# Loading order at the start of two stages of a hybrid decoder step: channel constants laid out on the host, weights in column halves, rows and tables ahead of the rest

## What is computed

```python
# layer 0: top-k sparse attention and retention side by side
qa, ka, va, iq, ik, iw, za, qb, kb, vb, zb = ab_project(rmsnorm(ys, norm_w[layer]), pos_s, w_in_ab[j])
oa = dsa_sample(qa, ka, va, iq, ik, iw, cache_k[j], cache_v[j], cache_kidx[j], page_table, topk_s)
ob, r_new = retention_chunked(qb, kb, vb, state_ret[j])
ys = ys + ab_output(oa, za, ob, zb, gn_ret[j], w_out_ab[j])
...
# layer 1: projection, causal convolution of width 4, gated delta rule
qkv, z, a, b = _split(h @ w_in, C_SIZES)
qkv, conv_new = causal_conv(qkv, conv_prefix, conv_w)
...
o = rmsnorm(o, gdn_norm) * jax.nn.silu(z.reshape(Bn, T, C_V_HEADS, C_V_DIM).astype(F32))
y = o.reshape(Bn, T, C_WIDTH).astype(h.dtype) @ w_out
```

## Time and profile before

| | us |
|---|---|
| median of 3 runs | 4261.64 |
| lowest, highest | 4259.95, 4264.33 |
| the profiled execution's own time | 4269.43 |
| its span | 4267.8 |
| PE busy | 3495.6 (82%) |
| DVE busy | 1880.5 (44%) |
| ACT busy | 1390.1 (33%) |
| POOL busy | 860.0 (20%) |

### The profile page before, as it was taken

How to read it: one execution, slowest core, us unless ns; L and a number is a source line. 1 busy time by engine, 2 the same in 40 slices (tenths; PEclk the granted TensorE clock), 3 DMA queues, 4 the chain that set the end, 5 groups by cost and what they waited for, 6 DMA issues and landing times. The chain is left out here.

```text
span 4267.8 us, 47903 instructions
## 1 busy us (share of the span) xinstructions
PE 3495.6 (82%) x15465; PEld 2026.5 (47%) x15465; DVE 1880.5 (44%) x3884; ACT 1390.1 (33%) x2831; POOL 860.0 (20%) x1709
## 2 busy tenths in 40 slices
PE   7999548899898988866538978979989864997998
PEld 4445334455555555653214434434434444665665
DVE  0000056677777775326400331521502436674664
ACT  2111135566565756522101111111111113442442
POOL 3112253221121100000000000000000004775572
PEclk9999778999999996877768989989989886998999
DMA  7333225454333320024041011010110113322321
GB/s 238 103 107 121 89 88 163 146 156 128 113 118 104 107 63 3 3 83 168 0 175 55 29 50 49 27 61 34 33 58 32 46 38 111 103 85 86 127 75 60
DMA packets 239806, 366.62 MB, mean 86 GB/s; under 512 B 54628, under 2 KB 139661, under 8 KB 235437
## 3 DMA queue, kind: packets, MB, share of 16 engines
q1 hardware_dynamic: 215920, 334.62, 24.2%
q10 hardware_dynamic: 19584, 21.05, 1.4%
q0 software_dynamic: 4096, 8.40, 0.7%
HBM read 279.22 MB, written 106.04 MB: 90 GB/s over the span
## 5 line engine op out<-in xcount | busy, mean ns | idle before, releaser
L1898 PE MATMUL QB<-hT,w_c 128*128 128x512 f32 (+1 forms) x1280 | 480.0, 529 | 0.0
L328 PE MATMUL P0A<-w_all,hT 128*128 128x512 f32 (+1 forms) x1200 | 432.9, 522 | 0.0
L631 PE MATMUL PB<-wb,hT_ahead 128*128 128x512 f32 x704 | 367.1, 648 | 3.4 <-ACT prb L751 1.9
L655 PEld LDWEIGHTS PO<-vst,ptT 128*128 128x128 f32 x2176 | 294.8, 207 | 81.0 <-issue 43.1
L1898 PEld LDWEIGHTS QB<-hT,w_c 128*128 128x128 f32 x1280 | 220.3, 191 | 218.1 <-issue 218.1
L655 PE MATMUL PO<-vst,ptT 128*128 128x64 f32 x2176 | 308.3, 287 | 13.4 <-ACT ptT L771 13.1
L328 PEld LDWEIGHTS P0A<-w_all,hT 128*128 128x128 f32 x1200 | 207.9, 191 | 220.5 <-issue 220.5
L2148 POOL TENSOR_SCALAR stat<-stat 128x1 f32<-128x1 f32 x17 | 3.3, 191 | 1438.6 <-POOLq L120 1438.6
L1864 PE MATMUL QS<-w_o,yT 128*128 128x512 f32 x544 | 277.3, 674 | 11.5 <-ACT yT L1996 11.5
L642 PE MATMUL PT<-ident,sm 128*128 128x128 f32 x1088 | 198.2, 308 | 106.1 <-ACT sm L763 105.9
L1887 PE MATMUL QA<-w_c,hT 128*128 128x512 f32 (+1 forms) x816 | 274.6, 493 | 9.3 <-ACT hT L2011 9.3
(11 more groups left out here) (404 smaller groups left out, 5253.0 us busy)
## 6 DMA issues: line engine op xcount, KB each, us to landing
wb<-in_w_in_ab SPq DMA_DIRECT2D x176, 512.0 KB, 3.7
out_c_all<-crow SPq DMA_DIRECT2D x272, 64.0 KB, 1.7
w_c<-in_w_in_c ACTq DMA_DIRECT2D x8, 1544.0 KB, 17.8
w_all<-in_w_in_ab SPq DMA_DIRECT2D x48, 256.0 KB, 8.0
out_pr_all<-pr_out SPq DMA_DIRECT2D x17, 546.0 KB, 2.9
pra<-out_pr_all SPq DMA_DIRECT2D x16, 546.0 KB, 4.6
x_rows<-in_x_all SPq DMA_DIRECT2D x17, 512.0 KB, 6.0
yab<-out_yab_all SPq DMA_DIRECT2D x17, 512.0 KB, 3.8
```

The costliest lines, as they stand in the source:

```text
L328: ins = pe.matmul(PA[u % 6][:, 0:b - a], hT[:, t % (LAG + 2), c, :], w_all[:, c, a:b], start=(c == 0), stop=(c == KD - 1))
L631: ins = pe.matmul(PB[:, :], hT[:, 2 * q + k, :], wb[:, u % 4, k, :], start=(q == 0 and k == 0), stop=(q == 3 and k == 1))
L655: ins = pe.matmul(PO[:, h * HD:(h + 1) * HD], ptT[:, v % 2, k * P:(k + 1) * P], vst[:, 4 * c + k, a * HD:(a + 1) * HD], start=(c == 0 and ...
L1898: ins = pe.matmul(PB[b % 2][:, 0:N], w_c[:, c, b * P:(b + 1) * P], hT[:, c, 0:N], start=(c == 0), stop=(c == KD - 1))
```

## The change

In the sample stage the rows, the two rotary tables and the identity are loaded first, under a semaphore of their own (rows4_loaded); PE, ACT and DVE start on that. The index blocks follow, then the other 12 constants under c4_loaded, for which DVE now waits after rope4 (the scaling of gng moves there too), and PE before its attention scores.

In the conv stage the host hands over nw1, gn and cw in the layout of their tiles. They are loaded first with ident, then yab and xin of sub-tile 0, then w_o in 16 pieces: eight for the left 512 columns (w2o_loaded0), eight for the right (w2o_loaded1). ACT waits for the right half and issues w_c in 16 pieces: the gate columns (w2z_loaded), then the rest (w2c_loaded). SP's sub_in(T) becomes next_in(T), which loads yab and xin of sub-tile T+1 as soon as T has used the buffers, ahead of the stores of T.

```diff
@@ layer0_samples, sync
+            rows = ((pr[:, :], io["pr_all"][SEQ:ROWS, :]),
+                    (ropea.rearrange("p a h d -> p (a h d)"), io["ropea"][SEQ:ROWS, :]),
+                    (ropeb.rearrange("p a d -> p (a d)"), io["ropeb"][SEQ:ROWS, :]), (ident[:, :], io["ident"]))
...
+            for dst, src in rows:
+                sp.dma_start(dst, src).then_inc(S["rows4_loaded"], 16)
@@ layer0_samples, tensor and scalar
-            pe.wait_ge(S["c4_loaded"], after(16 * N_CONST4))
+            pe.wait_ge(S["rows4_loaded"], after(64))
             pe.wait_ge(S["rope4"], after(1))
...
-            act.wait_ge(S["c4_loaded"], after(16 * N_CONST4))
+            act.wait_ge(S["rows4_loaded"], after(64))
@@ layer0_samples, vector
-            dve.wait_ge(S["c4_loaded"], after(16 * N_CONST4))
-            link(dve.tensor_scalar(gng, gng, 0.5, None, ALU.mult))
+            dve.wait_ge(S["rows4_loaded"], after(64))
...
             dve.sem_inc(S["rope4"], 1)
 
+            dve.wait_ge(S["c4_loaded"], after(16 * (N_CONST4 - 4)))
+            link(dve.tensor_scalar(gng, gng, 0.5, None, ALU.mult))
             dve.wait_ge(S["zeroed4"], after(2))
@@ layer0_out_and_conv, sync
-            for c in range(KD):
-                sp.dma_start(w_o[:, c, :], io["w_out_ab"][c * P:(c + 1) * P, :]).then_inc(S["w2o_loaded"], 16)
-            for dst, src in ((ident, io["ident"]),
-                             (nw1, io["norm_w"][1:2, :].rearrange("a (c p) -> p (a c)", p=P)),
-                             (gn, io["gdn_norm"].partition_broadcast(P))):
-                sp.dma_start(dst[:, :], src, allow_slow_non_contiguous=True).then_inc(S["c2_loaded"], 16)
-            for k in range(CONV):
-                sp.dma_start(cw[:, k, :], io["conv_w"][k:k + 1, :].rearrange("a (c p) -> p (a c)", p=P),
-                             allow_slow_non_contiguous=True).then_inc(S["c2_loaded"], 16)
-
-            def sub_in(T):
-                sp.wait_ge(S["yT_ps"], after(2 * T))
-                sp.dma_start(yab[:, :], io["yab_all"][ds(T * P, P), :]).then_inc(S["yab2_loaded"], 16)
-                sp.wait_ge(S["y1_ready"], after(2 * T))
-                sp.dma_start(xin[:, :], io["x_all"][ds(T * P, P), :]).then_inc(S["x2_loaded"], 16)
+            for dst, src in ((ident[:, :], io["ident"]), (nw1[:, :], io["norm1_t"]), (gn[:, :], io["gdn_rows"]),
+                             (cw[:, :, :].rearrange("p k b -> p (k b)"), io["conv_t"])):
+                sp.dma_start(dst, src).then_inc(S["c2_loaded"], 16)
+            sp.dma_start(yab[:, :], io["yab_all"][0:P, :]).then_inc(S["yab2_loaded"], 16)
+            sp.dma_start(xin[:, :], io["x_all"][0:P, :]).then_inc(S["x2_loaded"], 16)
+            for n in range(2):
+                for c in range(KD):
+                    sp.dma_start(w_o[:, c, n * 512:(n + 1) * 512], io["w_out_ab"][c * P:(c + 1) * P, n * 512:(n + 1) * 512])\
+                      .then_inc(S["w2o_loaded%d" % n], 16)
+
+            def next_in(T):
+                sp.wait_ge(S["yT_ps"], after(2 * T + 2))
+                sp.dma_start(yab[:, :], io["yab_all"][ds(T * P + P, P), :]).then_inc(S["yab2_loaded"], 16)
+                sp.wait_ge(S["y1_ready"], after(2 * T + 2))
+                sp.dma_start(xin[:, :], io["x_all"][ds(T * P + P, P), :]).then_inc(S["x2_loaded"], 16)
...
                     if s < n:
-                        sub_in(G * GT + s)
+                        if n > 1:
+                            next_in(G * GT + s)
                         sub_out(G * GT + s)
@@ layer0_out_and_conv, tensor
                 for n in range(2):
+                    pe.wait_ge(S["w2o_loaded%d" % n], after(16 * KD))
                     for c in range(KD):
...
-                pe.wait_ge(S["w2c_loaded"], after(16 * KD))
+                pe.wait_ge(S["w2z_loaded"], after(16 * KD))
...
-            pe.wait_ge(S["w2o_loaded"], after(16 * KD))
-            pe.wait_ge(S["c2_loaded"], after(16 * 7))
+            pe.wait_ge(S["c2_loaded"], after(16 * 4))
@@ layer0_out_and_conv, scalar
-            act.wait_ge(S["w2o_loaded"], after(16 * KD))
+            act.wait_ge(S["w2o_loaded1"], after(16 * KD))
             for c in range(KD):
-                act.dma_start(w_c[:, c, :], io["w_in_c"][c * P:(c + 1) * P, :]).then_inc(S["w2c_loaded"], 16)
-            act.wait_ge(S["c2_loaded"], after(16 * 7))
+                act.dma_start(w_c[:, c, CC:CIN], io["w_in_c"][c * P:(c + 1) * P, CC:CIN]).then_inc(S["w2z_loaded"], 16)
+            for c in range(KD):
+                act.dma_start(w_c[:, c, 0:CC], io["w_in_c"][c * P:(c + 1) * P, 0:CC]).then_inc(S["w2c_loaded"], 16)
+            act.wait_ge(S["c2_loaded"], after(16 * 4))
@@ kernel, host
+    arrays["norm1_t"] = np.ascontiguousarray(inp["norm_w"][1].reshape(KD, P).T)
+    arrays["gdn_rows"] = np.ascontiguousarray(np.broadcast_to(inp["gdn_norm"].reshape(1, P), (P, P)))
+    arrays["conv_t"] = np.ascontiguousarray(inp["conv_w"][0].reshape(CONV, NBLK, P).transpose(2, 0, 1).reshape(P, CONV * NBLK))
```

More of the change, by code:

```diff
@@ L1209 @@
     c4_loaded const4 exp4 gr4 gs4 iS_ps iS_sb isc4 iw_ps kd4 kt_ps kt_sb0 kt_sb1 mb4 new_out nm4 oall4 og4
-    pt4_ps pt4_sb pv4 q4_ps qbm4 qkb4 qm4 ra4_ps ra4_sb ret4_done ro4_ps rope4 rs4_upd rs_loaded rs_stored
-    s4_mx s4_ps s4_sb stage0 stage1 su4_ps tails4 tanh4 v4_0 v4_1 vm4 vt4 w4 wsel4 ya4 yab4 zeroed4 zeroed5"""
+    pt4_ps pt4_sb pv4 q4_ps qbm4 qkb4 qm4 ra4_ps ra4_sb ret4_done ro4_ps rope4 rows4_loaded rs4_upd rs_loaded
+    rs_stored s4_mx s4_ps s4_sb stage0 stage1 su4_ps tails4 tanh4 v4_0 v4_1 vm4 vt4 w4 wsel4 ya4 yab4 zeroed4
+    zeroed5"""
 CONV_SIGNALS = """
@@ L1214 @@
     cvh_ready cvt_ready hT2_ps hT2_sb hn2_ready pre_kept pre_loaded pre_ps pre_ready raw_ready rstd2_ready
-    ss2_ready tail_kept w2c_loaded w2o_loaded x2_loaded y1_ps y1_ready y1_stored yT_ps yT_sb yab2_loaded
-    z_free z_ps zg_ready zg_stored zt_ready"""
+    ss2_ready tail_kept w2c_loaded w2o_loaded0 w2o_loaded1 w2z_loaded x2_loaded y1_ps y1_ready y1_stored yT_ps
+    yT_sb yab2_loaded z_free z_ps zg_ready zg_stored zt_ready"""
 DELTA_SIGNALS = """
@@ L1314, in _ @@
         def _(sp):
-            consts = ((ident[:, :], io["ident"]), (hm[:, :, :].rearrange("p b t -> p (b t)"), io["hm"]),
+            rows = ((pr[:, :], io["pr_all"][SEQ:ROWS, :]),
+                    (ropea.rearrange("p a h d -> p (a h d)"), io["ropea"][SEQ:ROWS, :]),
+                    (ropeb.rearrange("p a d -> p (a d)"), io["ropeb"][SEQ:ROWS, :]), (ident[:, :], io["ident"]))
+            consts = ((hm[:, :, :].rearrange("p b t -> p (b t)"), io["hm"]),
                       (rep[:, :], io["rep"]), (rep4[:, :], io["rep4"]), (tmask[:, :], io["tmask"]),
@@ L1319, in _ @@
                       (qdec.rearrange("p c b t -> p (c b t)"), io["qdec_s"]), (kdec, io["kdec_s"]),
[L1320 to L1323, removed]
+                      (cdec, io["cdec_s"]), (bsel, io["bsel"][:, 0:DB]), (gng, io["gn_ret"].partition_broadcast(P)))
+            for dst, src in rows:
+                sp.dma_start(dst, src).then_inc(S["rows4_loaded"], 16)
             def index_in(i):
@@ L1339, in _ @@
                 sp.dma_start(dst, src, allow_slow_non_contiguous=True).then_inc(S["c4_loaded"], 16)
-            assert len(consts) == N_CONST4
             sp.wait_ge(S["zeroed4"], after(2))
@@ L1480, in _ @@
             pe.wait_ge(S["mb4"], after(1))
+            pe.wait_ge(S["c4_loaded"], after(16 * (N_CONST4 - 4)))
             pe.wait_ge(S["zeroed5"], after(3))
@@ L1892, in blocks @@
                 N = n * P
+                pe.wait_ge(S["w2c_loaded"], after(16 * KD))
                 for b in range(NBLK + 2):
@@ L2125, in _ @@
             dve.memset(tails[:, :, :], 0.0).then_inc(S["const2_ready"], 1)
-            dve.wait_ge(S["c2_loaded"], after(16 * 7))
+            dve.wait_ge(S["c2_loaded"], after(16 * 4))
             dve.tensor_scalar(cw[:, :, :], cw[:, :, :], 0.5, None, ALU.mult).then_inc(S["const2_ready"], 1)
```

## The result

| us | before | after |
|---|---|---|
| median (4 runs each) | 4262.99 | 4174.19 |
| lowest to highest | 4259.95 to 4265.84 | 4168.92 to 4175.66 |
| profiled execution's own time | 4269.43 | 4174.99 |
| its span | 4267.8 | 4173.5 |

The ratio is 0.9785, 95% interval [0.9773, 0.9797]: 88.8 us less by the medians, 94.4 by the two profiled executions. Predicted were 85.3 us and 4176.

The account below looks back on a forecast made before the run. PE's idle holes were taken as the bound. Gains of 10.3 (sample stage), 25.3 (conv start), 30.0 (group starts) and 19.7 (later sub-tiles) sum to 85.3 us; 4261.64 less that gives 4176 us, range 4160 to 4196.

Parts of the forecast that it names:

- What bounds the kernel: Whole kernel: PE works 82% of the span, so time is won where it stands idle; yab waits total 130.4 us.
- Sample stage: Sample stage's start: rows loaded first bring DVE's first evacuation forward, 10.3 us gained, bounds 7 to 11.7.
- Conv stage's start: Conv stage up to the first w_o matmul: 25.3 us gained, bounds 24.7 to 27.3, clock charge of 1.3 included.
- The loop, group starts: Starts of later groups: earlier yab loads close three waits of 10.0 us, 30.0 us gained, bounds 27 and 33.
- The loop, third and fourth sub-tile: Eight yab waits, 35.0 us in all, shrink to 1.91 each for hT: 19.7 us gained, bounds 15 and 26.
- I take no such gain: Loop's third and fourth sub-tiles: nothing counted for PE's clock keeping its level over the shorter wait.
- Held-up issues: Conv stage's start: ACT's 16 issues are held up by a full queue, giving 4180 or 4200 us; chance 0.15.
- issues cost nothing: Conv stage's start: ACT's issues do not hold its copies, 15 us more gain, 4161 us; chance 0.08.
- no other wait took the place of yab's: Loop: rival that another wait, likely ACT's or the residual, replaces yab's; only 35.6 us gained, 4226; chance 0.08.
- The constants did hold the stage: Conv stage's start: rival that w_c, not the constants, held it; 25.3 us of gain lost, 4201; chance 0.03.
- the clock falls in dense work: Dense convolution blocks: with fewer pauses PE might get 1.2 GHz, kernel slower, 4298 in one case; chance 0.03.
- Signs: Trace: yab waits under 10 us, eight hT waits near 1.9, first w_o matmul at 26 to 27, wsel waiting for wcol.

Follow-up runs that it names:

- samples_only: The kernel before with the sample stage's change alone: 4256.54 us against 4264.73, ratio 0.9979.
- whole_loads: The changed kernel with w_o and w_c loaded whole, 8 and 8 DMAs, everything else kept: 4170.68 us, ratio to before 0.9779.
- pool_issues: The changed kernel with w_c's 16 issues and the wait for w_o's right half moved from ACT to POOL: 4160.57 us, ratio to before 0.9759.
- layout_only: The kernel before with only the host's layout of nw1, gn and cw, load order and loop as before: 4233.51 us against 4264.73, ratio 0.9924.
- pool_whole_w_o: The changed kernel with w_c's issues and the wait for w_o on POOL, and w_o loaded whole in 8 DMAs: 4167.92 us, ratio to before 0.977.
- no_wait: The changed kernel without ACT's wait for w_o, so w_c is issued from the conv stage's first moment: 4185.27 us, ratio to before 0.9809.

## Why the prediction was right, point by point

- **What bounds the kernel.** Right: three holes in PE's work, and no other part moved. The tile's list of waits (12 times, 130.4 us) was the key; 58 of the 94 us between the two traces come from the loop, which the change's name does not mention.
- **Sample stage.** The steps held closely: DVE 7.7 us behind the first DMA (said 7.6), PE 11.6 earlier (11.7), gn_ret covered by PE's transposes (DVE waits 5.37 us for it, and then still 0.8 for PE at qm), wcol late, DVE's first evacuation 10.0 earlier (10.3). At the stage's end 8.7 are left in this pair of traces, 8.2 by samples_only's medians. Over all traces it is 7.6, with traces of the same stage up to 5 us apart. All three lie in the bounds of 7 to 11.7; the term may have been a little too large, and no run shows where the difference lies.
- **Conv stage's start.** The mechanism was right: ACT's wait for the right half and its 16 issues stand ahead of its copy, and the first matmul comes right behind them. The sizes: issues 9.2 us for 9.0; 1.1 from copy to matmul for 1.5; no charge for the clock where I took 1.3 (16.89 us for the 32 matmuls, 16.98 before); and w_o in at 18.6 us where I said 16.3. So the matmul stood at 29.2 where my working has 28.1, charge included, and the gain of 24.1 lies just outside its bounds of 24.7 to 27.3. Two parts of the landing time failed. The view of stretches of the changed kernel shows both (last column GB/s):

```profile
2158.00:2162.00 4.00, 0.00 (x0) 0.00 (x0) 0.64 (x5) 0.00 (x0) 0.00 (x0) 0.50 0.42 82
2162.00:2166.00 4.00, 1.96 (x8) 1.57 (x8) 0.74 (x1) 0.00 (x0) 0.00 (x0) 0.50 0.97 344
2166.00:2170.00 4.00, 0.00 (x0) 0.00 (x0) 0.00 (x0) 0.00 (x0) 0.00 (x0) 0.50 0.99 348
2170.00:2174.00 4.00, 0.00 (x0) 0.00 (x0) 0.00 (x0) 0.00 (x0) 0.00 (x0) 0.50 1.05 400
```

  The first is the rate of the halves. I took between 375 and 423 GB/s; the two stretches from 2166 on, when yab and xin were through, had 348 and 400. With whole rows (whole_loads) the stretches have 404 to 421, and w_o is in 1.6 us earlier. The second is the start-up. I carried 2.8 us over from a start that opens with w_o, 244 GB/s in its first 4 us. Here four small constants, 164 KB in 1.8 us of issues, stand ahead of the first large load, and the first 4 us have 82 GB/s; whole_loads has 74, and its w_o is in at 17.0 us where 423 GB/s and 2.8 us give 15.6. The Trainium skill's warning against DMAs under 1 MB (DMA: Bandwidth & Descriptors, Bandwidth), which I had set aside, gives nearly the measured time: by it my estimate was 2.4 us later, the measured time was 2.3 later. That is partly luck. Its table is for DMAs that GpSimd issues, and pieces of 512 KB, also under 1 MB, moved 404 to 421 GB/s in whole_loads, above the 341 that it has for 1 MB. Only the direction, smaller pieces slower, agrees.
- **The loop, group starts.** Predicted 3 x 10.0. From the last blocks' transposes to the first matmul with w_o it took 13.75 us before (2504.41 in the earlier trace rows to 2518.16) and 3.46 after (2461.74 to 2465.20), 10.3 each. Up to the second sub-tile's transposes another 0.6 and 0.7 came at two of the three starts, since turn_h now runs at the high clock there; at the one in the middle it had done so before. That is 32.2 in all, inside the bounds of 27 to 33.
- **The loop, third and fourth sub-tile.** Predicted 19.7, measured 25.7: in the first group, from turn_h to the gate matmuls, 23.4 us before and 20.1 after at the third, 24.6 and 21.5 at the fourth. The lines of before, beside those of the earlier trace rows:

```profile
2306.31 15.59 PE L1887 MATMUL QA<-w_c,hT 128*128 128x512 f32 x48
2321.75 1.07 PE L1874 MATMUL QT<-ident,hn 128*128 128x128 f32 x8
2329.92 16.61 PE L1864 MATMUL QS<-w_o,yT 128*128 128x512 f32 x32 [0.68 <-ACT yT L1996]
```

  The wait was sized well, 1.83 for 1.91: the eight shorter waits make 20.4 of the 25.7. What failed is "I take no such gain", which put the clock's part at nothing; it is the other 5.3. With the shorter wait PE's clock keeps its high level through the third sub-tile's transposes, 1.09 us for 1.96, and in the fourth the w_o matmuls run 16.1 us for 16.5. It was inside the bound of 26.
- **Rivals.** Held-up issues did not come (ACT's first eight took 3.97 us, the second eight 5.22). That issues cost nothing did not come either: they took the 9.2 us. But I priced this rival wrongly. I let PE start with the left half of w_o, though ACT would still wait for the right half; without the issues alone the first matmul comes 9 us earlier, which by the prediction's own terms is 4167, not 4161. What 4161 prices is pool_issues, where the wait leaves ACT too: 13.4 us instead of 29.2, and 4160.57. The lower end of the range rested on that price. The loop's gain came, so no other wait took the place of yab's. The constants did hold the stage: layout_only. That the clock falls in dense work did not come: the 48 matmuls of z_proj took 15.59 us as before, and the blocks as long as before.
- **Signs.** Two of those I named came otherwise: the first w_o matmul stood at 29.2 us, not 26 to 27 (that left out the clock's charge), and yab's waits fell to 20.6, not under 10, because the stage's first load is still waited for. The waits on hT (1.82 and 1.83 us), the place behind ACT's 16th issue and wsel's wait for wcol came as said.
- **Luck.** The loop was 8.5 us more than said, the start and the sample stage 2.8 less, so the three stretches give 91.0 us where I had 85.3. The medians give 88.8, and the median of the kernel before is 1.4 us above the one I started from. The changed median came 2 us from the forecast because such errors partly cancelled with each other and with the spread between runs.

## What to carry to other kernels

Look for the list of waits of one tile before reading what a change says of itself: a load issued behind stores in the loop was worth more here than both stage starts. When a stage opens with loads, follow the first matmul back through every engine's queue; an engine that must copy something for it should neither wait for weights nor issue them. Small one-element pieces in one DMA queue hold everything behind them (36 us here for 8192 numbers), and laying a constant out on the host removes that. Ask of each load that is moved ahead, or split, whose wait ends last: with ACT waiting for all of w_o, rows first and halves cost 10 us of the layout's 34 (layout_only); with ACT free, halves gained 3.8 (pool_whole_w_o).

## What the runs showed of the hardware that I had not expected

- Two queues with much to move did not share by bytes. With w_c (12.65 MB) on ACT's queue and w_o in pieces of 2 KB rows on SP's, both from the stage's start (no_wait), SP needed 29.1 us to issue 16 DMAs (8.3 in the changed kernel) and w_o's left half, 2.1 MB behind 1.2 MB, landed at 36.2 us instead of 13.4. The engines moved 415 GB/s from 7.7 to 32.7 us of the stage; of their bytes in the first 43 us SP's queue had 4.18 MB, ACT's 12.63. Whether they took turns by packets or SP's issues came late, no run separates.
- A wait of 1.82 to 1.83 us kept PE's granted clock at its high level in the transposes of the third sub-tile of every group (1.09 us) and not in those of the fourth (1.87 to 1.93). In the first group the granted clock was 0.86 in the 3 us from 2249 and 0.55 in the 3 us from 2285. The operations around both are the same, but what PE had done before differs: the w_o matmuls ahead of the third took 16.8 to 16.9 us, so part of them ran at the lower level, and those ahead of the fourth 15.5. Whether that is the cause no run shows.
- The part after the last mark (the rest of the samples' sub-tile and the stage layer1_delta) takes 864 to 866 us in eight of the profiled executions and 871 to 875 in five, though no version changes its loads or its work.
